# Who issues a third of the expert weight loads in a two-layer mixer and expert kernel

## What is computed

```python
aff = softmax(h @ w_router)                      # tokens x 16
gate, idx = top_k(aff.T, cap)                    # 64 latent + 16 context tokens per expert
xs = h[idx]                                      # 80 rows of 1024 per expert
y = (silu(xs @ w1[e]) * (xs @ w3[e])) @ w2[e] * gate
out = zeros.at[idx].add(y)
```

## Time and profile before

| | |
|---|---|
| median of 3 runs | 2993.83 us (2991.87 to 3005.42) |
| the profiled execution: its own time | 2993.84 us |
| its span, from first to last instruction | 2992.0 us |
| TensorE busy / VectorE / ScalarE / GpSimd | 93% / 39% / 23% / 13% of the span |
| mean granted TensorE clock | 0.972 of full speed |
| bytes moved by DMA | 608.08 MB, mean 203 GB/s over the span |

### The profile page before, as it was taken

The page is one execution under the profiler, slowest core; times in us unless marked ns, Lnnn a source line. Parts: engine busy times, 40 slices in busy tenths (PEclk is TensorE's granted clock), DMA queues, the critical chain, the costliest instruction groups (busy, mean ns, idle before and its releaser), DMA issues.

```text
span 2992.0 us, 70745 instructions
## 1 busy us (share of the span) xinstructions
PE 2784.9 (93%) x32716; PEld 2047.5 (68%) x32716; DVE 1179.4 (39%) x1655; ACT 689.3 (23%) x900; POOL 378.9 (13%) x356
## 2 busy tenths in 40 slices
PE   7999999999996999899889999999999869999996
PEld 3555576655753898888745556766566459988895
DVE  3973223332115443333469532233311344433335
ACT  2012023331003232322220120333310113232331
POOL 1330000000001121111125110000000011111111
PEclk9999999999997999999999999999999979999998
DMA  8222301012037999999932221012021359999994
GB/s 356 89 120 113 128 29 62 34 72 108 28 141 286 395 403 396 406 406 405 360 134 113 101 87 60 34 62 87 29 92 74 123 212 385 408 399 400 407 413 174
DMA packets 55634, 608.08 MB, mean 203 GB/s; under 512 B 6464, under 2 KB 6592, under 8 KB 21216
## 3 DMA queue, kind: packets, MB, share of 16 engines
q1 hardware_dynamic: 41504, 555.76, 45.9%
q0 software_dynamic: 7168, 23.47, 3.2%
q10 hardware_dynamic: 6848, 27.27, 2.3%
HBM read 577.25 MB, written 29.23 MB: 203 GB/s over the span
## 4 chain that ended last, share of the span: by engine, by line
PE 66%; DMA 24%; DVE 6%; ACT 2%; issue 2%; POOL 0%; DVEq 0%; ACTq 0%; POOLq 0%
PE ps L417 56%; DMA region_b<-in_w_exp 22%; DVE ring L1530 2%; ACT ring L1230 1%; DMA region_b<-in_w_last 1%; PE ps L702 1%; PE ps L685 1%; PE ps L759 1%; PE ps L740 1%; DVE rstd L1261 1%; PE ps L673 1%; DMA region_b<-h_rows,rstd 1%; PE ps L492 0%; PE ps L606 0%; PE ps L925 0%
## 5 line engine op out<-in xcount | busy, mean ns | idle before, releaser
L417 PE MATMUL ps<-hT,ring 128*128 128x320 f32 (+2 forms) x3480 | 986.4, 441 | 9.3 <-ACT hT L979 9.3
L417 PE MATMUL ps<-region_r,ring 128*64 128x80 f32 x24192 | 902.9, 236 | 68.0 <-ACT ring L1230 41.4
L417 PEld LDWEIGHTS ps<-region_r,ring 128*64 128x64 f32 x24192 | 880.0, 139 | 90.9 <-issue 52.9
L417 PEld LDWEIGHTS ps<-hT,ring 128*128 128x128 f32 x3480 | 591.0, 191 | 358.0 <-issue 225.9
L417 PE MATMUL ps<-region_b,ring 128*128 128x320 f32 (+2 forms) x896 | 257.4, 439 | 2.7 <-issue 2.7
L1329 DVE SCALAR_TENSOR_TENSOR region_b<-region_b,params 128x655 f32<-128x655 f32 x240 | 245.6, 1023 | 8.5
L1530 DVE COPY ring<-region_b 128x4096 f32<-128x4096 f32 x66 | 152.6, 2312 | 222.0 <-DMA region_b<-in_w_exp 109.2
L417 PEld LDWEIGHTS ps<-region_b,ring 128*128 128x128 f32 x896 | 159.3, 191 | 74.7 <-issue 26.9
L1230 ACT ACTIVATE ring<-region_b 128x4096 f32<-128x4096 f32 x28 | 101.3, 3620 | 265.6 <-DMA region_b<-in_w_exp 248.9
L1460 DVE TENSOR_TENSOR sig<-ps,sig 128x640 f32<-128x640 f32 x32 | 26.4, 825 | 323.1 <-PE ps L759 323.1
L417 PE MATMUL ps<-region_x,ring 128*128 128x512 f32 (+1 forms) x480 | 139.4, 449 | 3.8 <-DVE region_x L1464 3.8
(11 more groups left out here) (232 smaller groups left out, 2465.4 us busy)
## 6 DMA issues: line engine op xcount, KB each, us to landing
region_b<-in_w_exp SPq DMA_DIRECT2D x90, 2048.0 KB, 18.5
ring<-in_w_mix SPq DMA_DIRECT2D x61, 2048.0 KB, 9.4
hT<-in_w_exp SPq DMA_DIRECT2D x46, 2048.0 KB, 18.6
region_x<-in_w_exp SPq DMA_DIRECT2D x44, 2048.0 KB
ring<-in_w_ada SPq DMA_DIRECT2D x6, 2048.0 KB, 10.0
ring<-in_w_first SPq DMA_DIRECT2D x6, 2048.0 KB, 8.6
x_store<-region_m ACTq DMA_DIRECT2D x2, 2560.0 KB, 11.0
ffn_rows<-region_r ACTq DMA_DIRECT2D x4, 1280.0 KB, 17.6
```

The costliest lines, as they stand in the source:

```text
L417: ins = pe.matmul(*args, **kw)
```

## The change

ScalarE issues 28 of the 93 staged loads of a layer, on its own DMA queue. `ACT_LOADS` holds the blocks 13, 16, ..., 94, that is every third block from the one whose stage ScalarE's first copy (block 9) leaves. After its copy of block n ScalarE waits until that copy is complete (`slot_loaded`) and issues the load of block n + 4 into the same stage. SP leaves these blocks out, and still takes all others in the order of n. Nothing else changes: the same blocks go to the same stages and slots, the same engines copy them, and the same semaphores count them. The function that names the source of a block moves out of SP's program, so that both can call it.

```diff
--- before.py
+++ after.py
@@ -111,6 +111,18 @@
     return sum(name != "ada" for name, _ in TILES[0][:TILE_AT[0][phase, m] + 1])
 
 
+
+ACT_LOADS = [FIRST_BLOCKS + 3 * i + 2 + SLOTS + STAGES for i in range(HALVES - 2)]
+ACT_LOADS = [_n for _n in ACT_LOADS if _n < EXP_BLOCKS * NE]
+
+
+def expert_source(a, l, n):
+    if n < FIRST_BLOCKS:
+        return a["w_first"][l, n]
+    n -= FIRST_BLOCKS
+    return a["w_exp"][l, n // 3, n % 3] if n < LOOP_BLOCKS else a["w_last"][l, n - LOOP_BLOCKS]
+
+
 def staged_before(l, n):
 
     return l * -(-(EXP_BLOCKS * NE - SLOTS - (n - SLOTS) % STAGES) // STAGES) + (n - SLOTS) // STAGES
@@ -363,19 +375,13 @@
             for l in range(LAYERS):
                 need = needs(sp, l)
 
-                def expert_block(n):
-                    if n < FIRST_BLOCKS:
-                        return a["w_first"][l, n]
-                    n -= FIRST_BLOCKS
-                    return a["w_exp"][l, n // 3, n % 3] if n < LOOP_BLOCKS else a["w_last"][l, n - LOOP_BLOCKS]
-
                 def load_stage(n):
                     if n >= SLOTS + STAGES:
 
                         before = EXP_AT[l] + n - STAGES
                         sp.wait_ge(slot_loaded[before % SLOTS], 16 * (first_in_slot(before) + 1))
                     at = (n - SLOTS) % STAGES
-                    sp.dma_start(stage[at], expert_block(n)).then_inc(stage_in[at], 16)
+                    sp.dma_start(stage[at], expert_source(a, l, n)).then_inc(stage_in[at], 16)
 
                 for n in range(len(MIX_ORDER[l])):
                     load(MIX_AT[l] + n, a[f"w_mix{l}"][n])
@@ -388,12 +394,13 @@
                     for n, b in enumerate(NEXT_ADA):
                         load(BLOCK_AT[1][b], a["w_ada"][n])
                 for n in range(SLOTS):
-                    load(EXP_AT[l] + n, expert_block(n))
+                    load(EXP_AT[l] + n, expert_source(a, l, n))
                 need("h2_turned", TT)
                 load_stage(SLOTS + 2)
                 need("h2_stored", 16 * TT)
                 for n in range(SLOTS + 3, EXP_BLOCKS * NE):
-                    load_stage(n)
+                    if n not in ACT_LOADS:
+                        load_stage(n)
 
                 last = EXP_AT[l] + EXP_BLOCKS * NE - 2
                 sp.wait_ge(slot_loaded[last % SLOTS], 16 * (first_in_slot(last) + 1))
@@ -1229,6 +1236,9 @@
                         sc.wait_ge(slot_used[slot], first_in_slot(EXP_AT[l] + n) + 1)
                         sc.activation(ring[:, slot * 4096:(slot + 1) * 4096], stage[at], ACT.Copy)\
                             .then_inc(slot_loaded[slot], 16)
+                        if n + STAGES in ACT_LOADS:
+                            sc.wait_ge(slot_loaded[slot], 16 * (first_in_slot(EXP_AT[l] + n) + 1))
+                            sc.dma_start(stage[at], expert_source(a, l, n + STAGES)).then_inc(stage_in[at], 16)
                 for j in range(HALVES - 3, HALVES):
                     scale_y(j)
```

## The result

| | before | after |
|---|---|---|
| median (12 runs each) | 2994.3 us (2989.75 to 3005.42) | 3000.89 us (2995.95 to 3007.24) |
| ratio | | 1.0025, 95% interval 1.0013 to 1.0037 |
| profiled execution, and its span | 2993.84, 2992.0 us | 3000.49, 2998.7 us |

What follows compares the result with a forecast made beforehand. The prediction took the DMA engines as the bound. Its sum was 2993.84 + 0 for SP + 0 for ScalarE + 0 for the queue + 2 for the two ends = 2995.8, so 2996 us, range 2981 to 3026.

Steps and rivals of the forecast that it cites:

- The bound: Expert part: the DMA engines limit it, share 1.01 at 403 GB/s, with TensorE only 1.3 us a half behind.
- SP's order and issues: SP in the expert part: no load freed earlier, 56 fewer issues of 0.33 us lie under busy DMA; worth 0.
- The rival of 18.5 us saved: SP's issues: if their 0.33 us were on the path, 56 fewer save 18.5 us, time 2975; chance 0.02.
- ScalarE's work: ScalarE behind its copies: each load costs 0.54 us, 56 of them 30 us, covered by 10.3 us idle; worth 0.
- The second queue: Inside the expert stretch: ScalarE's load overtakes a block, but the engines stay busy at the same rate; worth 0 per half.
- Equal turns: DMA engines with both weight queues filled: turns of one packet each, so half the rate for each queue.
- The landing of ScalarE's loads: ScalarE's queue in the expert part: about 11 us from issue to landing, SP's at about 20 or more.
- run dry: Rival, DMA engines in the expert part: SP's queue empties before a release, up to 1.4 us each, 3072; chance 0.08.
- The end of the part: End of each layer's expert part: block 94's product begins 1 us late; 2 us for two layers.
- The lateness of block 93: End of the part: overtaken by block 94's load, block 93 lands by 1463.2 at the latest instead of 1458.5.
- the landing of block 95: End of the part: block 95 lands last, by about 1468 as before, since the bytes are the same.
- The rival of ScalarE's delay: ScalarE: idle time falls wrongly, Silu or scatters late, scatters get one turn in three; 30 us, time 3024; chance 0.07.

Runs made afterwards that it cites:

- the delay alone: Kernel before, SP loading all blocks, with ScalarE waiting for its copy and issuing a 4 KB DMA behind the same 28 copies a layer: 1.0000 of the kernel before.
- block 94 alone: ScalarE issues only the load of block 94 in each layer, SP all others as in the kernel before: 1.0011 of the kernel before.
- the last four loads: ScalarE issues only the loads of blocks 85, 88, 91 and 94 in each layer, SP all others: 1.0015 of the kernel before.
- the early loads alone: Changed kernel with 24 of 28 loads a layer kept on ScalarE's queue and 85, 88, 91, 94 back on SP: 0.9997 of the kernel before.
- the kernels with ScalarE's order changed: ScalarE copies block 93 behind half 28's scaling: with only block 94's load on ScalarE 1.0019; with VectorE's order changed too, kernel before 1.0014, changed kernel 1.0054.
- both orders: ScalarE copies block 93 behind half 28's scaling, VectorE copies block 95 behind half 31's product: on the kernel before 1.0014, on the changed kernel 1.0054.

## Why the prediction held, and where it was off

**The bound: right.** The DMA share of 1.01 and 402 GB/s after the change, and the time saved without scatters (36 us of the 46 expected), show it.

**SP's order and issues, worth 0: right.** The rival of 18.5 us saved didn't come.

**ScalarE's work, worth 0: right.** 0.47 us from copy to Silu where 0.45 was forecast, covered by a pause of 10 us, and 1.0000 with the delay alone.

**The second queue, worth 0 inside the stretch: right within what can be told.** Equal turns were a choice ahead of the result; the shares of 52.0 and 49.0% bear it out. The landing of ScalarE's loads was put too early, at 11 us for 13.6 to 14.6. The engines didn't run dry. With 24 loads on the second queue the ratio was 0.9997.

**The end of the part: the place right, the term mis-sized.** It was put at 1 us a layer, 2 in all; the runs show 3.9 to 11 in all for the whole change. TensorE's own way, the one that the prediction followed, was some 2.8 us late in all by the estimate above, close to its 2; the rest is the way of the summed rows, on which TensorE then waited 4.13 and 3.85 us. The lateness of block 93 was about what was forecast, 5.2 and 3.2 us in after where 4.7 was the limit. Two things were missing behind it. First, the prediction followed block 93 only through TensorE to `copy_y` and block 94's product. It did not follow what is queued behind the copy on ScalarE: the scaling of half 28, its scatter, the load of the summed rows. With block 94 alone this moves the summed rows by 4.6 us in the mean of the layers. Second, block 90 wasn't looked at. It is 7.8 and 7.2 us late in after, and through the scatter of the last full expert it holds up the same scaling; with the last four loads the summed rows come 3.4 and 4.5 us later though block 93 is nearly on time. With 94 alone TensorE's side, too, came out above 1 us: block 94's product began at 1471.14 - 957.86 = 513.28 us behind the first load, against 1472.04 - 962.20 = 509.84, so 3.4 us late, of which 1.5 are the slower product of block 93. The prediction also held the landing of block 95 fixed. In after VectorE copied it as it landed, 3.5 and 2.3 us later than before, and with the early loads alone 2.7 and 1.4 later.

**The rival of ScalarE's delay named a mechanism that was there.** Its price of 30 us was wrong, but its second half, that scatters get a smaller share and `scale_y` waits, is seen: 37.1 us of waits, ten of them, in after, and none in before. Inside the stretch they cost nothing that can be told, by the early loads alone, and the one at the end of each part stands in the chain.

**Open.** The early loads' 1.4 to 3 us in the distances; how the lateness of the summed rows divides between block 90 and block 93 when both are late; whether the changed kernel without scatters still loses; and what brought TensorE's clock down in the first layer of the kernels with ScalarE's order changed.

## What to carry to other kernels

Where the DMA engines were busy all the time, a second queue brought no bytes sooner: it only changed which block came first, and a block asked for later that overtook took its time from those that were needed before it. That cost nothing that could be told in the middle (24 of 28 loads, 0.9997) and something at the end (the last four, 1.0015), where no later block fills in. For a delay at the end, follow every engine's program behind the late instruction, not only the one that seems to be the bound.

## What the hardware showed that was not expected

Order changes that looked free cost time, through TensorE's pauses and its clock: 1.0014 for the kernel before with both orders, and 1.0054 for the changed kernel with them, against 1.0025 without. A pause of 4.3 to 4.8 us before a block's products was followed by 6.1 to 6.2 us for them instead of 4.57. In the three kernels with ScalarE's order changed, the twenty products that come some 20 us later in the first layer took 10.5 to 10.9 us instead of 6.47; in one of them a window of 15 us had a granted clock of 0.56, a mean between the levels of 1.2 and 2.4 GHz near the lower, where the kernel before had 1.00.

The pause is not shown to be the cause of that second slowing. With 94 alone TensorE stood 4.59 us and took 6.07 for the block, and yet the twenty took 6.47; and in the kernel before without scatters, whose order is unchanged, they took 10.88. The second layer has 6.47 in all three.
